# A diffusion trunk on one core: TensorE's transposes and values ahead of the next unit's scores in both attentions

## The reference

```python
# layer 0: four heads, two maps each, tokens and context as queries
s = jnp.einsum('bqhmd,bkhmd->bhmqk', qi, k).astype(jnp.float32) * scale
p = jnp.einsum('bhmqk,m->bhqk', jax.nn.softmax(s, axis=-1), w)
o = jnp.einsum('bhqk,bkhd->bqhd', p.astype(v.dtype), v)
# layer 1, heads C (eight, with a position bias and a mask on the local keys)
p = jax.nn.softmax(jnp.concatenate([s_loc, s_ctx], axis=-1), axis=-1)
# layer 1, heads D (four, latent attention): blocked_attention with one map
```

## Time and profile before

| | |
|---|---|
| median of 3 runs | 2241.19 us (2237.32 to 2241.66) |
| span of the profiled execution | 2240.4 us, its own time |
| TensorE busy | 2015.4 us, 90% |
| VectorE busy | 1433.3 us, 64% |
| ScalarE busy | 1210.4 us, 54% |
| attention 0, first score to last value | 265.07 to 322.16 us |
| attention 1, first score to last value | 1007.85 to 1096.32 us |

### The profile page before, as it was taken

The page is one execution under the profiler, slowest core; times in us unless marked ns, Lnnn a source line. Parts: engine busy times, 40 slices in busy tenths (PEclk is TensorE's granted clock), DMA queues, the critical chain, the costliest instruction groups (busy, mean ns, idle before and its releaser), DMA issues.

```text
span 2240.4 us, 25373 instructions
## 1 busy us (share of the span) xinstructions
PE 2015.4 (90%) x9386; PEld 1603.1 (72%) x9386; DVE 1433.3 (64%) x1355; ACT 1210.4 (54%) x1227; POOL 68.4 (3%) x124
## 2 busy tenths in 40 slices
PE   4699778699999977878979999999999999999996
PEld 3587546488887846853768878788787878878785
DVE  3545473633323336455458888888888888888885
ACT  3644353433322236433537767676777777776773
POOL 0011000000000000113000000000000000000000
PEclk9899889899999988986959999999999999999998
DMA  8455202143332214521028989899998989899891
GB/s 277 149 170 174 72 1 75 38 151 125 122 112 94 94 38 146 190 81 31 22 94 330 365 308 368 307 362 336 348 361 307 367 313 364 323 353 361 314 364 51
DMA packets 266582, 473.49 MB, mean 211 GB/s; under 512 B 19416, under 2 KB 119056, under 8 KB 266512
## 3 DMA queue, kind: packets, MB, share of 16 engines
q1 hardware_dynamic: 262928, 469.33, 59.5%
q0 software_dynamic: 3456, 3.19, 0.6%
q10 hardware_dynamic: 128, 0.03, 0.0%
HBM read 471.27 MB, written 1.05 MB: 211 GB/s over the span
## 4 chain that ended last, share of the span: by engine, by line
PE 79%; DVE 11%; ACT 5%; issue 3%; DMA 1%; ACTq 0%; SPq 0%; DVEq 0%; POOL 0%
PE bank L478 22%; PE bank L479 22%; PE bank L480 22%; PE bank L527 2%; PE bank L646 2%; DVE split_low L462 2%; ACT split_high L457 2%; PE bank L347 2%; DVE overlay L371 2%; PE bank L1657 2%; DVE split_low L1421 2%; ACT overlay L406 1%; PE bank L621 1%; PE bank L1699 1%; PE bank L636 1%
## 5 line engine op out<-in xcount | busy, mean ns | idle before, releaser
L1421 DVE TENSOR_TENSOR split_low<-raw_weights,split_high 128x2048 fp32r<-128x2048 f32 x224 | 511.7, 2287 | 59.8 <-ACT split_high L1115 58.8
L1115 ACT ACTIVATE split_high<-raw_weights 128x2048 fp32r<-128x2048 f32 x224 | 429.3, 1920 | 147.7 <-PE bank L480 147.7
L462 DVE TENSOR_TENSOR split_low<-raw_weights,split_high 128x1024 fp32r<-128x1024 f32 x214 | 256.9, 1224 | 372.2 <-ACT split_high L457 372.1
L478 PE MATMUL bank<-h_high,split_high 128*128 128x512 f32 (+1 forms) x848 | 329.3, 388 | 47.6 <-DVE h_low L392 30.5
L457 ACT ACTIVATE split_high<-raw_weights 128x1024 fp32r<-128x1024 f32 x214 | 219.5, 1051 | 227.9 <-PE bank L480 210.8
L479 PE MATMUL bank<-h_low,split_high 128*128 128x512 f32 (+1 forms) x848 | 322.8, 381 | 0.0
L480 PE MATMUL bank<-h_high,split_low 128*128 128x512 f32 (+1 forms) x848 | 322.7, 381 | 0.0
L1421 DVE TENSOR_TENSOR h_low<-raw_weights,h_high 128x2048 fp32r<-128x2048 f32 x112 | 256.7, 2292 | 78.7 <-ACT h_high L1115 78.6
L478 PE MATMUL bank<-split_high,xe_high 128*128 128x512 f32 x672 | 272.2, 405 | 14.0 <-DVE split_low L1421 14.0
L479 PE MATMUL bank<-split_low,xe_high 128*128 128x512 f32 x672 | 267.6, 398 | 0.0
L480 PE MATMUL bank<-split_high,xe_low 128*128 128x512 f32 x672 | 265.2, 395 | 0.0
(11 more groups left out here) (242 smaller groups left out, 3028.9 us busy)
## 6 DMA issues: line engine op xcount, KB each, us to landing
raw_weights<-in_moe_w SPq DMA_DIRECT2D x336, 1024.0 KB, 6.6
raw_weights<-in_w_mod SPq DMA_DIRECT2D x48, 1024.0 KB, 5.3
raw_weights<-in_ffn_w SPq DMA_DIRECT2D x33, 1024.0 KB, 5.2
raw_weights<-in_ev_w_in SPq DMA_DIRECT2D x10, 1024.0 KB, 5.8
raw_weights<-in_od_w_in SPq DMA_DIRECT2D x8, 1024.0 KB, 5.6
raw_weights<-in_ev_w_out SPq DMA_DIRECT2D x4, 1024.0 KB, 5.5
raw_weights<-in_od_w_out SPq DMA_DIRECT2D x4, 1024.0 KB, 5.3
overlay<-in_rpb SPq DMA_DIRECT2D x32, 64.0 KB, 2.3
```

The source lines that it names most:

```text
L462: dve.tensor_tensor(half_of(s, j, SPL[:, s % NSPLIT, :]), half_of(s, j, raw_of(split_at[s])), half_of(s, j, SPH[:, s % NSPLIT, :]).bitcast ...
L478: pe.matmul(ps, wh, xh, start=first, stop=False)
L1115: act.activation(esplit(u)[0], RAW[:, u % NRAW, :], ACT.Copy).then_inc(S("e_high"), 1)
L1421: dve.tensor_tensor(lo, RAW[:, u % NRAW, :], hi.bitcast(F32), ALU.subtract)\
```

## The change

In TensorE's loop the scores of unit i+1 are issued at the end of pass i and no longer at its start. Before, pass i was S of unit i+1, T of unit i-1, and, where i is odd, V of the pair that ended with unit i-2. After, it is T, V, S. The scores of the first two units still come ahead of the loop. Nothing is added or removed, and the other engines' loops, the waits, the buffers and the transfers are the same.

```diff
@@ -625,8 +625,6 @@
             scores(0)
             scores(1)
             for i in range(1, len(units) + 2):
-                if i + 1 < len(units):
-                    scores(i + 1)
                 if i <= len(units):
                     u = units[i - 1]
                     pe.wait_ge(S(f"prob{a}"), i)
@@ -646,6 +644,8 @@
                         last = pe.matmul(pair_out(units, p)[0], u["v"][kt], PT[p % 2][:, kt, :],
                                          start=(kt == 0), stop=(kt == u["nk"] - 1))
                     last.then_inc(S(f"o{a}"), 1)
+                if i + 1 < len(units):
+                    scores(i + 1)
 
         def act_attention(act, a, units):
```

## The result

The changed kernel takes 2335.82 us, median of 4 runs (2332.47 to 2336.45), beside 2240.69 us of before on the same chip: a ratio of 1.0416, 95% interval 1.04 to 1.0433. It is 95 us slower; 2337 us was forecast, in a range of 2292 to 2360. The profiled execution took 2332.47 us, with a span of 2330.6.

A forecast was written before the change was run, and what follows sets the result against it. No one engine bounds the attentions throughout: VectorE sets attention 0's pace, TensorE is busiest in attention 1. Profiled 2240.4 us plus 96.3 us (46.8 plus 0.7 x 70.7) gave 2337 us, range 2292 to 2360.

The forecast's parts named there:

- The closed loop: Both attentions: VectorE's M and P and TensorE's T, V, S run without overlap; a head takes 18.2 to 25.1 us.
- The handovers allowed: Gaps between VectorE and TensorE in the loop, estimated at 0.24 us a unit, four or five of 0.03 to 0.06 us.
- The starts and the ends: M of unit 2 starts 1.9 us later in attention 0, 1.0 in attention 1; nothing changes behind attention 0's last M.
- The three costs: Attention 0 loses 22.5 to 44.9 us, attention 1's units with bias 14.6 to 44.7, those without 9.7 to 27.9.
- seven tenths of the way from full to half clock: Chosen TensorE clock share in both attentions, between 46.8 us at full and 117.5 at half: a cost of 96.3 us.
- One remark on the clock: Claim that in the trace of before the TensorE clock sank inside both attentions; no size given.
- The clock mostly up: Rival: the same serial loop in the attentions with TensorE's clock mostly full, 2287 us, up to about 2305; chance 0.2.
- The clock down nearly throughout: Rival: the serial loop in the attentions with the clock low nearly throughout, 2350 to 2358 us; chance 0.1.
- Left-over cover: Rival: part of the overlap stays, for example S overlapping the end of V, 2250 to 2287 us; chance 0.06.
- No effect, because attention 1 at half clock is TensorE's own work: Rival: TensorE's work fills 9.77 of a pair's 10.19 us, so order would not matter, 2240 us; no-effect chance 0.03.
- No effect, by matmuls that pass a waiting T: Rival: TensorE takes ready scores ahead of the waiting T, so nothing is lost, 2240 us; no-effect chance 0.03.
- Faster: Rival: T no longer stands behind S, ending VectorE's 21.1 us wait in attention 1, 2220 us; chance 0.02.

The follow-up runs named there:

- the stalls filled: Changed kernel plus three unread filler matmuls behind each score in attention 1, in TensorE's stall: 2306.36 us, ratio 1.0289; attention 1 113.01 us.
- the runs above: Attention 1 with fillers in its stalls: the changed order took 113.01 us, the order of before (scores, transposes, values) 78.57 us.
- S, V, T: Kernel of before with the values moved ahead of the transposes in both attentions, scores still first: 2242.1 us, ratio 1.0007.
- S, T, V: Attention 1 keeps the order of before; attention 0 alone has the values ahead of the transposes, no fillers: 2237.66 us, ratio 0.9984.
- S, V, T and fillers only ahead: Values ahead of transposes in both attentions, filler matmuls ahead of attention 1 but none inside its passes: 2239.63 us, ratio 0.9986 to before.
- the clock held at full: Values ahead of transposes in both attentions, fillers ahead of attention 1 and inside its even passes: 2225.43 us, ratio 0.9929 to before.

## Why the prediction was right, step by step

**The closed loop.** Right. M(i), P(i-1), T(i-1), V, S(i+1) follow each other without overlap. A pair with bias at half clock was put at 14.0 us and took 14.28; at full clock at 9.7, and took 9.61 with the stalls filled; a pair without bias at full clock at 7.9, and took 7.92; a head, at a clock of 0.57, took 24.47 us between the bounds of 18.2 and 25.1. The handovers allowed were right to 0.3 us a pair; the 14.28 us lie just outside the 9.7 to 14 that were to show the loop.

**The starts and the ends.** M of unit 2 came 1.8 us later in attention 0 (forecast 1.9) and 0.9 us in attention 1 (1.0). Behind the last M nothing changed but the clock: attention 0's end took 9.3 us for 10.4.

**The three costs.** From M of unit 2 on, with its delay, attention 0 lost 41.0 us before its end (bounds 22.5 and 44.9), the units with bias 40.9 us (14.6 and 44.7), the units without bias 13.3 us (9.7 and 27.9), 95.2 us together. These starts are read from the timeline of the changed kernel:

```profile
350.71 1.29 DVE L705 TENSOR_REDUCE small<-bank 128x1 f32<-128x512 f32 x2 [2.46 <-PE bank L621]
```

```profile
1055.89 0.42 DVE L696 TENSOR_SCALAR y<-bank 128x256 f32<-128x256 f32 x1 [3.21 <-PE bank L621]
...
1150.10 0.69 DVE L705 TENSOR_REDUCE small<-bank 128x1 f32<-128x512 f32 x1 [6.09 <-PE bank L621]
...
1181.39 0.69 DVE L705 TENSOR_REDUCE small<-bank 128x1 f32<-128x512 f32 x1 [1.61 <-PE bank L621]
```

For example the units with bias: 1150.10 - 1055.89 = 94.2 us for 54.3, and 0.9 from their start. The lower bounds set the changed kernel at full clock against before as it ran, with 38 us at half clock in it; set against before at full clock, the loop's own price in attention 1 is higher, 34.4 us by the runs above.

**Where the clock stands.** The one choice in the sum, seven tenths of the way from full to half clock, came out nearly so: (95.2 - 46.8) / 70.7 = 0.68. But it was a choice, and that it came out is in part luck: one share for all was a coarse picture, and it was helped by cancelling. Attention 0 and the units with bias lay at 0.83 and 0.87 of their ways, the units without bias at 0.20, since the clock rose there. That the lower clock is a price of the stalls, and not a coincidence, is shown for attention 1 by the filled stalls; for attention 0 it is only argued from the row at 0.60. One remark on the clock was half right: it sank inside attention 0 of before, but attention 1 was entered at the lower level (0.50 from 1004 to 1008) and rose inside, at 1046. The Trainium skill (TensorE: Matmul & The Clock Gate, Part 1, "What's actually happening") says that throttled is the default and activity releases it; the filled stalls agree, 0.94 for 0.66.

**The rivals.** The clock mostly up: it would have given 2287 to 2305 us; the averages of 0.60 and 0.66 exclude it. The clock down nearly throughout, 2350 to 2358 us: the pair without bias at 1.00 excludes it. Left-over cover: none was found, only the small change in the end of attention 0. No effect, because attention 1 at half clock is TensorE's own work: at half clock the pair with bias went from 10.19 to 14.28 us. No effect, by matmuls that pass a waiting T: no S of the changed kernel starts before its T, even where it was ready (at 1103.02, and started at 1111.98). The row at 273.07, on which the prediction rests this, showed less, since there S was already running when P ended at 272.17. Faster: the wait of 21.1 us for T did go, and became 62.2 us for S, since M reads S.

**The remainder.** The forecast was 1.2 us above the median. The three terms less the 1.1 us of attention 0's end give 94.1 us in the profiled execution, and 3.9 us came back outside the attentions, where the edit does nothing; that execution was the fastest of the four. What those 3.9 us are was not tried.

## What to carry to other kernels

In a loop written by hand over several engines, do not read the time of an order off busy shares: write down the cycle of who waits for whom, and put on each engine's queue, ahead of an instruction that will wait, the work that is ready and that others need. Here the scores ahead of the waiting transposes were the only cover that VectorE's step had, and behind them each pass became the sum of both engines' work. Then price the clock separately, before the change and after it: with stalls of two microseconds a pass the lower TensorE clock was 29.6 of the 142.6 us of attention 1, some 10 of 88.5 before, and filler matmuls inside a stall, but only inside one, gave it back.

## What the runs showed of the hardware that was not expected

- The granted clock stayed at its lower level, 1.2 GHz, for 38 us in attention 1 of before, with TensorE at work for 34.29 us of them. With seventeen filler matmuls ahead of it and around its first scores and two in each stall, attention 1 ran at 0.98 to 1.00. Why it stayed low in the kernel before was not isolated.
- More work made the program faster: 66 additional matmuls took 29 us off the changed kernel, and 31 ahead of and inside attention 1 took some 17 us off S, V, T (ratio 0.9929 for 1.0007) and some 9 us off S, T, V there (0.9944 for 0.9984).
- The same kernel's attention takes different times as the clock happens to go: with S, V, T and fillers only ahead, the runs lay between 2232.09 and 2243.35 us, while with the clock held at full they lay between 2224.45 and 2226.79.
